# Where the low parts of a split-float32 two-block transformer are cut, with other tap counts, first banks, turn order and load order

## The reference, cut to what matters

```python
# layer 1: gated linear attention, then an MLP
h = rms_norm(x, g);  q, k, v, g, glr = split(h @ w_in)     # 3088 columns
log_a = log_sigmoid(glr @ w_gate_up + b) / 16               # chunks of 64 tokens
o = chunked_gla(q, k, v, log_a);  x += rms_norm((norm(o) * silu(g)) @ w_out)
x += rms_norm(square(relu(rms_norm(x) @ w_up)) @ w_down)    # 1024 -> 4096 -> 1024
# layer 2: sliding-window attention with sinks, 16 heads of 64, then the same MLP
# second block
z = rms_norm(x) @ w_in_2                                    # glu, q, k, v, gates: 7168 columns
a = depthwise_conv31(a_val * sigmoid(a_gate));  y_a = silu(rms_norm(a)) @ w_conv_out
y_b = dilated_attention(q, k, v) @ w_attn_out               # 16 heads, three dilations
x += (g_a * y_a + g_b * y_b) @ w_out
u = depthwise_conv3(rms_norm(x) @ w_up_2)                   # 2 * 2816 columns
x += (silu(u_gate) * u_val) @ w_down_2
```

## Time and profile before

| what | value |
|---|---|
| time, median of 3 runs | 2176.86 us (2174.45 to 2178.8) |
| the profiled execution's own time | 2175.81 us |
| its span | 2174.0 us |
| mean granted TensorE clock | 0.987 |
| HBM read | 181.13 MB |
| TensorE, VectorE, ScalarE, GpSimd busy | 2078.2, 1166.0, 881.7, 385.0 us |

### The profile page before, as it was taken

How to read it: one execution, slowest core, us unless ns; L and a number is a source line. 1 busy time by engine, 2 the same in 40 slices (tenths; PEclk the granted TensorE clock), 3 DMA queues, 4 the chain that set the end, 5 groups by cost and what they waited for, 6 DMA issues and landing times.

```text
span 2174.0 us, 25685 instructions
## 1 busy us (share of the span) xinstructions
PE 2078.2 (96%) x10072; PEld 1717.3 (79%) x10072; DVE 1166.0 (54%) x1581; ACT 881.7 (41%) x1442; POOL 385.0 (18%) x172
## 2 busy tenths in 40 slices
PE   5989999999999999999999999999989999999998
PEld 5778788878788888887878886777777778887876
DVE  3242654444454556443446687777802536995762
ACT  3332544233234654422324326776623334442331
POOL 0000200000000000000000142232463334443432
PEclk9999999999999999999999999999999999999999
DMA  4231123223224012322422321111032222232321
GB/s 171 66 107 39 68 69 106 97 78 126 88 78 153 32 49 78 105 98 69 136 78 80 110 97 54 49 49 49 30 106 80 95 78 97 97 97 88 101 93 58
DMA packets 49556, 184.89 MB, mean 85 GB/s; under 512 B 5500, under 2 KB 5628, under 8 KB 48797
## 3 DMA queue, kind: packets, MB, share of 16 engines
q1 hardware_dynamic: 49436, 183.25, 25.3%
HBM read 181.13 MB, written 2.10 MB: 84 GB/s over the span
## 4 chain that ended last, share of the span: by engine, by line
PE 88%; DVE 3%; ACT 3%; POOL 3%; issue 2%; DMA 0%; POOLq 0%; SPq 0%; ACTq 0%; DVEq 0%
PE ps L373 16%; PE ps L375 16%; PE ps L374 16%; PE ps L399 10%; PE ps L400 9%; PE ps L401 9%; POOL WL L1986 3%; PE ps L755 2%; PE ps L725 2%; PE ps L637 1%; PE ps L669 1%; ACT WH L882 1%; PE ps L421 1%; PE ps L739 1%; PE ps L652 1%
## 5 line engine op out<-in xcount | busy, mean ns | idle before, releaser
L373 PE MATMUL ps<-HH,WH 128*128 128x512 f32 (+1 forms) x1784 | 665.4, 373 | 25.4 <-DVE HL L1477 13.1
L374 PE MATMUL ps<-HL,WH 128*128 128x512 f32 (+1 forms) x1784 | 656.7, 368 | 0.0
L375 PE MATMUL ps<-HH,WL 128*128 128x512 f32 (+1 forms) x1784 | 656.5, 368 | 0.0
L1986 POOL TENSOR_TENSOR WL<-WR,WH 128x1024 fp32r<-128x1024 f32 x134 | 350.7, 2623 | 1502.8 <-ACT WH L882 1502.7
L882 ACT ACTIVATE WH<-WR 128x1024 fp32r<-128x1024 f32 x305 | 320.4, 1057 | 650.8 <-PE ps L375 350.0
L373 PEld LDWEIGHTS ps<-HH,WH 128*128 128x128 f32 x1784 | 338.9, 190 | 86.9 <-issue 27.1
L374 PEld LDWEIGHTS ps<-HL,WH 128*128 128x128 f32 x1784 | 339.3, 190 | 55.8 <-issue 1.9
L375 PEld LDWEIGHTS ps<-HH,WL 128*128 128x128 f32 x1784 | 338.7, 190 | 55.9
L1450 DVE TENSOR_TENSOR WL<-WR,WH 128x1024 fp32r<-128x1024 f32 x171 | 208.4, 1224 | 184.7 <-ACT WH L882 180.1
L399 PE MATMUL ps<-WH,HIDH 128*128 128x512 f32 x624 | 246.4, 395 | 19.5 <-DVE RT L1670 13.1
L400 PE MATMUL ps<-WH,HIDL 128*128 128x512 f32 x624 | 244.5, 392 | 0.0
(11 more groups left out here) (223 smaller groups left out, 2307.0 us busy)
## 6 DMA issues: line engine op xcount, KB each, us to landing
WR<-in_up SPq DMA_DIRECT2D x108, 512.0 KB, 3.5
WR<-in_down SPq DMA_DIRECT2D x86, 512.0 KB, 3.5
WR<-in_in SPq DMA_DIRECT2D x56, 512.0 KB, 3.4
WR<-in_swa_in SPq DMA_DIRECT2D x10, 512.0 KB, 4.0
WR<-in_gla_in SPq DMA_DIRECT2D x9, 512.0 KB, 6.8
WR<-in_gla_v SPq DMA_DIRECT2D x8, 512.0 KB, 3.5
WR<-in_gla_g SPq DMA_DIRECT2D x8, 512.0 KB, 5.1
GAIN<-in_gain SPq DMA_DIRECT2D x4, 1024.0 KB, 7.3
```

Source lines behind the costliest of these rows:

```text
L373: e.matmul(ps, wh, hi[:, c, cols], start=c == 0, stop=False)
L374: e.matmul(ps, wh, lo[:, c, cols], start=False, stop=False)
L375: y = e.matmul(ps, wl, hi[:, c, cols], start=False, stop=c == x.n - 1)
L1986: e.tensor_tensor(x.wl[:, 0:n], m.WR[:, u % RAW, 0:n], x.wh[:, 0:n].bitcast(F32), A.subtract).then_inc(*k.mark("wlop", u))
```

## The change

All low parts are cut by VectorE with `v_cut`; `g_cut` and the field `lo` are gone, and GpSimd keeps only its sums and products. In the second block `v_cut` calls are put into VectorE's program. The numbers taken by `more` differ. The MLP's second and third group of `down` begin with bank pair (2,3), as do the value product and the first gate product of layer 1 with other banks. `t_turn` of the last tile stands after the third instead of the fourth half product. In several places the order of a cut and an evacuation is exchanged. The first loads and the first norms come in another order.

```diff
-N_EARLY = CONST_AT["swam"][0]          # 641 columns
+N_EARLY = CONST_AT["ones"][0]          # "ident" and "eps", 129 columns
@@ t_starts
     for j in range(4):
-        product(e, k, u + j, m.HH, m.HL, 0, 2 + j, lambda c: [("hlo", tag, 1, 1)])
-    if tag == "mix0":
-        t_turn(e, k, tag, 2)
-    t_turn(e, k, tag, 3)
+        product(e, k, u + j, m.HH, m.HL, 0, 2 + j, lambda c: [("hlo", tag, 1, c // 4)])
+        if tag == "mix0" and j in (1, 3):
+            t_turn(e, k, tag, 2 + j // 2)
+        if tag != "mix0" and j == 2:
+            t_turn(e, k, tag, 3)
     for j in range(4):
-        product(e, k, u + j, m.HH, m.HL, 1, 2 + j, lambda c: [("hlo", tag, 3, 1)], evs[j])
+        product(e, k, u + j, m.HH, m.HL, 1, 2 + j, lambda c: [("hlo", tag, 3, c // 4)], evs[j])
@@ t_gla
-        tokens(e, k, v + 4 * q, 4, hi, lo, 4 * q, t, 2 * (p % 2), (("va", "v")[q], q, t))
+        tokens(e, k, v + 4 * q, 4, hi, lo, 4 * q, t, 2 * ((p + 1) % 2), (("va", "v")[q], q, t))
-    k.ring(0, 1, 2)
+    k.ring(0, 1, 2, begin=2)
@@ t_mlp
-        k.ring(0, 1, 2)
+        k.ring(0, 1, 2, begin=min(o, 1))
@@ a_gla (v_gla alike, with v_normed and v_split)
-    a_cut(e, k, u)
-    for t in range(4):
+    for t in range(2):
         a_mean(e, k, "pre", "mix0", t, m.X[:, t, :], (f"x_in{t}",))
-        if 1 <= t <= 2:
-            a_split(e, k, "mix0", t - 1)
-        a_cut(e, k, u + t)
-    a_split(e, k, "mix0", 2)
-    a_split(e, k, "mix0", 3)
+        a_split(e, k, "mix0", t)
+        if t == 0:
+            a_cut(e, k, u)
+    for t in range(2, 4):
+        a_cut(e, k, u + t - 1)
+        a_mean(e, k, "pre", "mix0", t, m.X[:, t, :], (f"x_in{t}",))
+        if t == 3:
+            a_cut(e, k, u + 3)
+        a_split(e, k, "mix0", t)
@@ a_gla, v_gla: evac_v and evac(8) ahead of the cuts of their step, and
-    a_cut(e, k, w + 5)
+    a_cut(e, k, w + 7)
     o_norm(1)
-    a_cut(e, k, w + 7)
@@ v_ends: the cut of following + 2 from t == 3 to t == 2
@@ a_second, v_second
-        if j > 4:
-            more(4)                      # glu
+        if j > 3:
+            more(5)
-        more(7)                          # in heads(i), and before norm_qk(c)
+        more(4)
-        more(4)                          # gates, 14 times
+        more(7)
@@ v_second: new calls, one cut each unless told
+        v_cut(e, k, u + 3)               # qkv: ahead of heads(2c-2), u + 4 ahead of
+        v_cut(e, k, u + 4)               # heads(2c-1), u + 5 behind it
+        v_cut(e, k, u + j + 3)           # gates: ahead of more(7)
+    v_cut(e, k, u + 6)                   # attn_out: three, behind evac_b(0..2)
+        v_cut(e, k, u + j + 3)           # attn_out, j = 4..7: behind evac_b(j-1)
+        if j == 0:
+            v_cut(e, k, u + 6)           # conv_out: three, behind evac_y(0)
+        elif 3 <= j < 7:
+            v_cut(e, k, u + j + 4)
@@ v_ffn
         later(j)
+        v_cut(e, k, u + 4)
+                if t == 3:
+                    v_cut(e, k, u + 7)   # downs: four, ahead of the last add
@@ scalar_program: the two operations on the parameters go to the start of a_swa
@@ sync_program: x0, const (129 columns), gains, x1, units 0 and 1, x2, unit 2, x3, unit 3,
   gate weights, the other constants, parameters
```

More of the change, by code:

```diff
@@ L158, in add @@
                 holds[s] = len(units)
-            units.append(Unit(t, size, lo, wh, wl, event))
+            units.append(Unit(t, size, wh, wl, event))
     def each(name, n):
@@ L180, in plan @@
     add("glu", [d["in2"][8 * (1 - j % 2) + j // 2] for j in range(16)])
[L181 to L187, removed]
+    add("qkv", [d["in2"][16 + 8 * j + c] for c in range(8) for j in range(3)])
+    add("gate", [d["in2"][40 + j] for j in range(16)])
+    add("attn_out", each("attn_out", 8))
+    add("conv_out", each("conv_out", 8))
+    add("out2", each("out2", 8), extra=m.EXTRA["second"], freed=("unit", at["conv_out"] + 7))
     ups = [d["up2"][j // 2 + FC2 * (j % 2)] for j in range(2 * FC2)]
-    add("fup_a", ups[:32], lo="wlop")
+    add("fup_a", ups[:32])
     down = each("down2", FC2)
[L191 to L194, removed]
+    add("fdown0", down[:8])
+    add("fup_b", ups[32:])
+    add("fdown1", down[8:16])
+    add("fdown2", down[16:])
     return units, at
@@ L472, in decays @@
         e.wait_ge(*k.on("la", 3))
+        e.wait_ge(*k.on("late"))
         e.wait_ge(*k.on(*k.free[b]))
@@ L1302, in a_second @@
         evac_qk(c, 1)
-        more(7)
+        more(4)
         norm_qk(c)
@@ L1842, in v_second @@
         evac_glu(j - 1)
-        if j > 4:
-            more(4)
+        if j > 3:
+            more(5)
     evac_glu(15)
     for c in range(8):
+        u = at["qkv"] + 3 * c
         if c:
             evac_v(c - 1)
+        v_cut(e, k, u + 3)
+        if c:
             heads(2 * c - 2)
+        v_cut(e, k, u + 4)
+        if c:
             heads(2 * c - 1)
-        more(7)
+        v_cut(e, k, u + 5)
+        more(4)
         norm_qk(c)
+    u = at["gate"]
     evac_v(7)
+    v_cut(e, k, u + 3)
     heads(14)
+    v_cut(e, k, u + 4)
     heads(15)
@@ L1857, in v_second @@
     for j in range(2, 16):
-        more(4)
+        v_cut(e, k, u + j + 3)
+        more(7)
     for c in range(8):
@@ L1881, in conv_out @@
                             A.subtract).then_inc(*k.mark("ol", c - 1))
+    u = at["attn_out"]
+    v_cut(e, k, u + 3)
     more(1000)
@@ L1973, in vector_program @@
     v_ffn(e, k)
-def g_cut(e, k, upto):
-    m = k.m
-    u = k.cut.get("lop", k.at["glu"] + 8)
-    while u <= min(upto, len(k.units) - 1):
-        x = k.units[u]
-        n = x.n * 128
-        e.wait_ge(*k.on("whi", u))
-        e.tensor_tensor(x.wl[:, 0:n], m.WR[:, u % RAW, 0:n], x.wh[:, 0:n].bitcast(F32), A.subtract).then_inc(
-            *k.mark("wlop", u))
-        u += 1
-    k.cut["lop"] = u
 def g_gla(e, k):
@@ L2017, in g_second @@
         taps.add(c)
-    for j in range(5, 16):
-        g_cut(e, k, at["glu"] + j + 3)
-        more(4)
-    for c in range(8):
-        u = at["qkv"] + 3 * c
-        for j in range(3):
-            g_cut(e, k, u + j + 3)
-            if c or j == 2:
-                more(7)
-    for j in range(2):
-        g_cut(e, k, at["gate"] + j + 3)
-        more(7)
-    for j in range(2, 16):
-        g_cut(e, k, at["gate"] + j + 3)
-        more(4)
-    g_cut(e, k, at["attn_out"] + 6)
     more(1000)
-    g_cut(e, k, len(k.units))
 def gpsimd_program(e, k):
```

75 lines of the change are left out of this document (40 added, 35 removed).

## The result

The kernel after takes 2108.24 us (median of 4 runs, 2106.17 to 2108.69); before took 2177.83 beside it. The ratio is 0.9681, with an interval of 0.9664 to 0.9698. Predicted were 2112.7 us and 2101 to 2133. The profiled execution took 2108.69 us with a span of 2106.9, against 2175.8 and 2174.0: 67.1 us less, where the sum had 64.2.

The account below looks back on a forecast made before the run. TensorE was taken as the bound, busy 2078 of 2174 us, leaving only its waits and slow clock to win. Terms summed to 64.2 off 2175.8, giving 2111.6; 1.1 more for the median made 2112.7, range 2101 to 2133.

Parts of the forecast that it names:

- closing products: MLP down groups: four TensorE waits for VectorE's evacuation go, with the slow clock behind them; 16.7 us won, bounds 13.1 to 16.7.
- last turn: Five openings after the start: TensorE's 1.66 us waits go as the turn moves 2.9 us ahead; 8.3 us won.
- layer 1: Four waits, at value product, fifth pass, first gate product and output product, shrink or go; 16.2 us won, bounds 8 to 17.
- start: First loads and norms: first turn at 8.8, first product at 18, new 3.2 us wait; 3.5 us won, bounds 1 to 6.
- feed-forward: Last feed-forward: ten 0.65 us waits for GpSimd's cuts go, with their restarts; 9.5 us won, bounds 6.5 to 9.5.
- gates: Gate products: TensorE's 5.7 us wait for a stretched GpSimd cut goes, with 2.1 of clock; 7.8 us won.
- attn_out's start: First attn_out product: VectorE's gate taps and cuts end later, TensorE waits 4.8 instead of 2.1; 3.0 us lost with clock.
- heads: Heads: four fast taps and a cut replace seven slow taps ahead of a reciprocal; 2.3 us won, bounds 0 to 4.
- convolution's norm: Second block: evac_b(7) ends 0.9 later behind three VectorE cuts, sums' squares cost 0.3; 1.3 us lost.
- The clock came back: Rival: about 17 us of slow stretches could persist in other places, total 2128; chance 0.10.
- A tap of VectorE in the gates: Rival: gate taps take 0.884 each, so the 94 need 20.7 us more ahead of attn_out's operand, total 2133; chance 0.08.
- VectorE did not become the bound: Rival: VectorE stays slow in glu, gates and feed-forward and bounds the kernel, 105 us more, total 2218; chance 0.03.

Follow-up runs that it names:

- a_taps: Kernel after with convolution taps moved from the gates to the heads (5 instead of 4 per call in heads, 6 instead of 7 in gates): 2097.74 us.
- a_ kernels: Kernels that are each the kernel after with one edit; measured times 2097.74 to 2110.11 us.
- c_all: Kernel after with four edits: taps moved to heads, attn_out's last four products in banks 5-7, 641 early constant columns, start cuts before splits: 2093.32 us.
- b_ kernel: Kernel before with one edit: closing products' first bank 2157.08 us, last turn one tile sooner 2167.36, VectorE cutting the last feed-forward 2169.59.
- a_lock: Kernel after with three added GpSimd multiplications (128x512, results unused), each released as seven unbroken gate taps follow on VectorE: 2110.11 us, one run.
- b_gap: Kernel before, with VectorE waiting for its own last tap after every four in the gates, cuts still on GpSimd: 2167.45 us.
- a_ring: Kernel after with attn_out's last four products in PSUM banks 5, 6, 7 instead of 0, 1, 2: 2098.24 us.
- a_pool: Kernel after with ten added GpSimd instructions (multiply, copy, memset; results unused) in glu, each released by a VectorE cut: 2108.24 us, one run.

## Why the prediction was right, term by term

| Part | predicted | measured |
|---|---|---|
| closing products | 16.7 | 18.5 |
| last turn | 8.3 | 9.4 |
| layer 1 | 16.2 | 19.0 |
| start | 3.5 | -0.4 in the pair of profiles, 2.5 as a mean of five each |
| feed-forward | 9.5 | 9.0 |
| gates | 7.8 | 9.6, of which 8.0 at the stretched cut |
| attn_out's start | -3.0 | -4.6 |
| heads | 2.3 | 4.0 |
| convolution's norm | -1.3 | -2.3 |
| y | 4.2 | 5.3 |

Measured is the difference of two distances in the profiles of before and after. The column adds to 67.5 with the start at -0.4; 0.4 of it is lost again in a place that no part covers.

Two pieces of the column are luck of the one profile of after. The slow stretch of before behind the last wait of the heads (2.7 us for L1256, L1250 in before), worth 1.6 us in the row of the gates, is absent in after and in a_taps. It is there in the other seven of the nine profiles of after, the a_ kernels and c_all, and all nine have that wait. The one at 238 us of before, worth 1.6 us in layer 1, is absent in four of the nine and there in five. Without these two, layer 1 and the gates stand at 17.4 and 8.0, close to what was counted. So these two add 3.2 us that no mechanism of the prediction gives, and the start, 2.9 short of its mean, took nearly as much away.

*Closings, turn, feed-forward.* Right in mechanism and nearly in size, each shown alone by its b_ kernel. The closings were short by 1.8: a row of 10 us at full clock counts 46 matmuls (449 to 459 above), where the sum had let 44.3 fit, so that 81 were missing in the four places and not 74. The turn won 1.9 at each of five openings instead of 1.66.

*Layer 1.* The mechanism was right at all four places, the two waits left over are 0.36 and 0.96 where 0.5 and 1.0 had been expected, and VectorE evacuates for the gate product at 134.93, ahead of the four cuts. The size was 2.8 short: the first place gave 6.2 instead of 5.2, and 1.6 is the slow stretch at 238 us, which none of the four waits explains. The other three places gave 3.2, 5.0 and 3.0 against 3.2, 4.9 and 2.9. No experiment took layer 1 apart, so this is read from the two profiles only.

*Gates and attn_out.* The gates' 8.0 is the 7.8 counted. At attn_out the term that was mis-sized is the new wait, 6.2 where I had 4.8. VectorE's 94 taps and 14 cuts took 80.2 us (1511.82 to 1591.97), not 78.6. The group beside GpSimd's four sums took 5.35 instead of 3.40, and I had left the sums out. a_taps and a_lock show that the wait is VectorE's load, and b_gap that the stretched cut caused the 5.7. The Trainium skill's rule that the port is locked for one instruction at a time (SBUF — State Buffer, "SBUF: two separate sides") fits the probes of a_lock, which take their turn in 1.67 to 1.75 us; it does not explain the 20.6 of the earlier trace rows. The reading of the row, not the rule, gave the sum.

*Heads, norm, y.* Right in kind. The heads won 3.0 at the place counted and 1.0 in small waits elsewhere. In the norm the wait of 4.0 was predicted to end 0.9 later and ended 1.4 later, at 5.4. a_ring shows it to be the bank, as predicted; VectorE's rows show three cuts in front of that evacuation, two of them idle for 1.1 us and one for 2.3 until ScalarE's cut ends. The sums of squares, counted at 0.3, cost 0.8. In y no lower clock stayed behind the last wait (0.8), where 1.0 of it had been left in the sum.

*The start* is the term that failed in the pair of profiles: -0.4 where 3.5 was summed. The new wait of 2.94 was predicted at 3.2 and is there. What was off: the gains' landing, taken as a fixed 7 us from the bytes, scatters from 6.4 to 9.2 between six profiles of one order of loads; and the lower clock, taken at 1.3 us ahead of that wait and 1.4 behind it, cost 1.8 and 2.8. In a_pool the first turn was at 8.71 and the first product at 17.81 (predicted 8.8 and 18), and the halves still began 1.6 late, by the clock alone.

*The rivals.* The clock came back: mean 0.994, against 0.987. A tap of VectorE in the gates took 0.67, not 0.88. VectorE did not become the bound: with 325 cuts instead of 187 it is busy 1176 us instead of 1166, because the steps beside GpSimd no longer take 1.2 to 1.8 us. The cuts add 164 us of rows on VectorE (208.4 to 372.0 for the full tiles), the 240 taps take 165.3 instead of 194.8, and the 88 three-tap steps 66.0 instead of 156.7.

## What to carry to other kernels

Work given to GpSimd can cost VectorE more than doing it itself: here a GpSimd cut took about 2.2 us from the VectorE instruction beside it, and VectorE's own cut takes 1.15. Moving 138 cuts to the busier engine added only 10 us to its busy time. Moving work also moves the end of that engine's chain, so look for the next operand that stands behind it, and give the last stretch before it the least side work. A GpSimd instruction that something waits for should not be released far into a long run of VectorE instructions without a pause. A wait put down to "issue" in front of a product is worth a trial with another bank. And of a start that hangs on loads, take several profiles before believing one.

## What the hardware showed that was not expected

- A GpSimd subtraction of 128x1024 took 20.6 us beside 42 unbroken taps and 2.4 to 3.0 us when VectorE waited for its own tap after each four. In the five traces of kernels that have such cuts beside taps, all 79 released in taps 1 to 6 of an unbroken run got in at the next tap, and all 24 released in taps 11 to 15 got in only behind the last one.
- On VectorE's side a 128x512 GpSimd instruction costs 0.65 to 1.04 us with two inputs, up to 0.35 as a copy, none as a memset.
- With the same loads in the same order a 512 KB load landed 4.7 to 7.5 us after its issue, in six profiles.
- Stretches at the lower granted clock, worth 1.6 to 3.2 us, come and go between profiles whose instructions there are the same: at 68 us in after, with no wait of 0.3 us or more from 42 to 111, and none there in a_taps and a_pool. A wait of 2.7 us in the heads had one behind it in seven of nine profiles.
